# Attention, sample attention, merge and output norm in one block, with SBUF places set by hand

## What is computed

```python
h = layer_norm(x)                                   # T = 2048 + 32 rows of 1024
x_a, B, C, z_a, q, k, v, f, z_b, merge = split(h @ w_in)
y_a = B * causal_depthwise_conv3(C * x_a) * silu(z_a)
logits[t, s] = q_t . k_s / 8 + sum of log f over s < j <= t, for s <= t   # 8 heads of 64
y_b = (softmax(logits) @ v) * silu(z_b)
mixed = sigmoid(merge_A) * (y_a @ w_proj_a) + sigmoid(merge_B) * (y_b @ w_proj_b)
y = layer_norm(2 ** 0.25 * h + mixed @ w_out)
```

## Time and profile before

| | us |
|---|---|
| median of 3 runs (lowest, highest) | 2121.68 (2120.96, 2125.2) |
| own time of the profiled execution | 2120.03 |
| its span, first to last instruction | 2117.9 |
| TensorE busy in it | 1912.2 (90%) |
| VectorE, ScalarE, GpSimd busy | 1267.0, 870.7, 402.9 |
| mean granted TensorE clock | 0.957 of full |

### The profile page before, as it was taken

How to read it: one execution, slowest core, us unless ns; L and a number is a source line. 1 busy time by engine, 2 the same in 40 slices (tenths; PEclk the granted TensorE clock), 3 DMA queues, 4 the chain that set the end, 5 groups by cost and what they waited for, 6 DMA issues and landing times. The chain is left out here.

```text
span 2117.9 us, 29147 instructions
## 1 busy us (share of the span) xinstructions
PE 1912.2 (90%) x10726; PEld 1750.7 (83%) x10726; DVE 1267.0 (60%) x2002; ACT 870.7 (41%) x1546; POOL 402.9 (19%) x301
## 2 busy tenths in 40 slices
PE   2999999999999999999976999999993869997997
PEld 2999999999999999999974777777772659996886
DVE  7688887944646555445436888888874322225544
ACT  4454545633434344233321766676672510003221
POOL 4000110000101000000000245444453322421222
PEclk9999999999999999999985999999996779998999
DMA  4588888969789878788857155555424379436441
GB/s 176 180 307 306 291 302 280 315 227 312 254 279 327 272 242 274 243 300 277 266 193 155 36 121 118 114 121 107 100 51 103 115 282 328 153 121 216 156 149 67
DMA packets 272981, 435.99 MB, mean 206 GB/s; under 512 B 63228, under 2 KB 139404, under 8 KB 268708
## 3 DMA queue, kind: packets, MB, share of 16 engines
q1 hardware_dynamic: 272852, 434.29, 64.5%
HBM read 285.31 MB, written 148.78 MB: 205 GB/s over the span
## 5 line engine op out<-in xcount | busy, mean ns | idle before, releaser
L621 ACT ACTIVATE fr_wq<-fr_raw 128x512 fp32r<-128x512 f32 x288 | 177.9, 625 | 198.1 <-PE fr_d L518 130.7
L1482 DVE TENSOR_TENSOR at_p_lo<-at_p,at_p_hi 128x512 fp32r<-128x512 f32 (+2 forms) x240 | 195.0, 819 | 55.3 <-ACT at_p_hi L1436 54.7
L1435 ACT ACTIVATE at_p<-at_s 128x512 f32<-128x512 f32 (+1 forms) x320 | 170.5, 533 | 108.6 <-PE at_s L1359 62.9
L516 PE MATMUL fr_a<-fr_xh,fr_wq 128*128 128x348 f32 x576 | 187.7, 326 | 18.9 <-ACT fr_p L717 17.1
L516 PE MATMUL fr_b<-fr_xh,fr_wq 128*128 128x348 f32 x576 | 188.8, 328 | 17.0 <-DVE fr_u L1007 14.6
L866 DVE TENSOR_TENSOR fr_wq<-fr_raw,fr_wq 128x512 fp32r<-128x512 f32 x288 | 192.7, 683 | 10.5 <-ACT fr_wq L621 6.7
L1489 DVE TENSOR_REDUCE at_piece_max<-at_m 128x1 f32<-128x512 f32 (+2 forms) x294 | 171.1, 603 | 37.1 <-PE at_m L1391 17.0
L516 PE MATMUL fr_c<-fr_xh,fr_wq 128*128 128x348 f32 x576 | 186.3, 323 | 1.4 <-DMA fr_wq<-w_mixed 1.4
L517 PE MATMUL fr_b<-fr_xl,fr_wq 128*128 128x348 f32 x576 | 186.7, 324 | 0.0
L517 PE MATMUL fr_a<-fr_xl,fr_wq 128*128 128x348 f32 x576 | 186.7, 324 | 0.0
L518 PE MATMUL fr_a<-fr_xh,fr_wq 128*128 128x348 f32 x576 | 186.7, 324 | 0.0
(11 more groups left out here) (303 smaller groups left out, 4821.4 us busy)
## 6 DMA issues: line engine op xcount, KB each, us to landing
fr_wq<-w_mixed SPq DMA_DIRECT2D x192, 512.0 KB, 5.5
fr_raw<-w_tiles SPq DMA_DIRECT2D x96, 512.0 KB, 5.4
w_mixed<-fr_wq SPq DMA_DIRECT2D x96, 512.0 KB, 4.3
mg_gates<-merge_gates SPq DMA_DIRECT2D x40, 416.0 KB, 4.1
fr_raw<-w_tiles SPq DMA_DIRECT2D x48, 256.0 KB, 5.5
merge_gates<-fr_res SPq DMA_DIRECT2D x32, 348.0 KB, 6.7
mixed<-mg_mixed SPq DMA_DIRECT2D x40, 208.0 KB, 2.8
ln_m<-mixed SPq DMA_DIRECT2D x16, 512.0 KB, 4.0
```

What stands on the lines that cost most here:

```text
L516: pe.matmul(to, wh[:, idx, k, :], xh[:, idx, k, :], start=first, stop=False, skip_group_check=skip)
L621: act.activation(wh[:, idx], operand(i, idx), ACT.Copy).then_inc(w_hi[idx], 1)
L1435: act.activation(p[:, r, cols], s_bank[r][:, cols], ACT.Exp, scale=SCALE)
L1482: dve.tensor_tensor(p_lo[:, r, cols], p[:, r, cols], p_hi[:, r, cols].bitcast(F32), ALU.subtract)\
```

## The change

The four stages become objects whose engine programs are called one after the other inside one block (`rest`), so no engine waits for all others between them; each wait is on the semaphore of what it needs. `Place` puts each buffer at an offset in SBUF, counted in float32 words, so that a stage's buffers lie where those of the one before are free: `k_rows` over attention's `main` of the even heads, `v_rows` over `k_rows`, and so on. PSUM banks are shared in the same way.

- Attention: GpSimd's part of `low` goes to VectorE, so GpSimd only finishes heads, without the waits for p_hi between. The last head's `scale`, `gate` and `lower` go from VectorE to GpSimd.
- SP loads the sample's small inputs in head 1 (`early_loads`) and the four pieces of K, all of them resident, in head 7 (`key_loads`). VectorE makes the sample's masks before head 1, GpSimd clears its queries at the start.
- `tail_loads` is SP's order from there on. V pieces are loaded when the K piece in their place is turned.
- The kT parts take two slots instead of whole buffers. Merge's item (0, 0, 0) is issued on TensorE before the sample's last transposes; merge's first weight splits stand inside the sample part.
- w_out is loaded and split during merge's second group, in two raw buffers; output uses four pairs of banks, four slots of m and no special first tiles. Loops are written out.

```diff
-    prompt_attention(nc, held, s, ident, causal)
-    sample_attention(nc, held, s, cache_k, cache_v, ident, causal, blocks)
-    merge(nc, held, s, wpa_tiles, wpb_tiles)
-    output_norm(nc, held, s, w_out, ln_out, y_prompt, y_sample)
+    rest(nc, held, s, cache_k, cache_v, ident, causal, blocks, wpa_tiles, wpb_tiles, w_out, ln_out, y_prompt, y_sample)
...
+class Place:
+    BASE = 16512
+    def __init__(self, nc, tag):
+        self.nc, self.tag = nc, tag
+    def __call__(self, name, shape, at, dt=F32):
+        return self.nc.alloc_sbuf_tensor_at(f"{self.tag}_{name}", list(shape), dt, offset=self.BASE + 4 * at)
+def rest(nc, held, s, cache_k, cache_v, ident, causal, blocks, wpa_tiles, wpb_tiles, w_out, ln_out, y_prompt, y_sample):
+    with ExitStack() as ctx:
+        att = prompt_attention(nc, held, s, ident, causal)
+        sam = sample_attention(nc, held, s, att, cache_k, cache_v, blocks)
+        mrg = merge(nc, held, s, att, sam, wpa_tiles, wpb_tiles)
+        out = output_norm(nc, held, s, mrg, w_out, ln_out, y_prompt, y_sample)
+        block = ctx.enter_context(nc.Block())
+        @block.sync
+        def _(sp):
+            att.sync(sp, sam)
+            tail_loads(sp, s, att, sam, mrg, out)
+        @block.tensor
+        def _(pe):
+            att.tensor(pe)
+            sam.tensor(pe, mrg)
+            mrg.tensor(pe)
+            out.tensor(pe)
+        @block.scalar
+        def _(act):
+            att.scalar(act)
+            sam.scalar(act, mrg)
+            mrg.scalar(act, out)
+            out.scalar(act)
+        @block.vector
+        def _(dve):
+            att.vector(dve, sam)
+            sam.vector(dve)
+            mrg.vector(dve, out)
+            out.vector(dve)
+        @block.gpsimd
+        def _(pool):
+            att.gpsimd(pool, sam)
+            sam.gpsimd(pool, mrg)
+            mrg.gpsimd(pool)
+            out.gpsimd(pool)
...
+        main = sb("main", [P, 2, 4, SEQ], 0, F32R)
+        km = sb("km", [HR, 3, SEQ], 16384, F32R)
+        qm = sb("qm", [HR, 3, SEQ], 22528, F32R)
...
-                pe.wait_ge(*low_value(h, st))
+                pe.wait_ge(lo_done, NS * h + st + 1)
...
+            for h in range(1, H):
                 for st in range(NS):
-                    if st % POOLS == POOLS - 1:
-                        low(h, st)
-                    if before and st in FINISH_LOW:
-                        lower(h - 1, 1 - b, FINISH_LOW[st])
-                    if before and st in FINISH and FINISH[st][1] < 2:
-                        (scale, gate)[FINISH[st][1]](h - 1, 1 - b, FINISH[st][0])
-            for h in range(H):
-                head(h, h % 2)
-def sample_attention(nc, held, s, cache_k, cache_v, ident, causal, blocks):
+                    if st in FINISH_LOW:
+                        lower(pool, h - 1, 1 - h % 2, FINISH_LOW[st])
+                    if st in FINISH and FINISH[st][1] < 2:
+                        (scale, gate)[FINISH[st][1]](pool, h - 1, 1 - h % 2, FINISH[st][0])
...
+        def key_loads(sp):
+            sp.wait_ge(*att.head6_done)
+            for c in range(NP):
+                sp.dma_start(k_rows[:, c], cache_k[c * PIECE:(c + 1) * PIECE, :].rearrange("(b p) c -> p b c", p=P))\
+                  .then_inc(k_in[c], 16)
+            for i in range(2):
+                sp.dma_start(ck[i * H:(i + 1) * H, :].bitcast(F32), s["ck"][i, :, SEQ:SEQ + PAST]).then_inc(past_in, 16)
+            sp.dma_start(pick32[:, :], blocks).then_inc(pick_in, 16)
+        def load_v(sp, c):
+            sp.wait_ge(turned, 4 * c + 4)
+            for d in (2 * c, 2 * c + 1):
+                sp.dma_start(v_rows[:, d], cache_v[d * 2 * P:(d + 1) * 2 * P, :].rearrange("(b p) c -> p b c", p=P))\
+                  .then_inc(v_in[d], 16)
...
+            h, b = H - 1, (H - 1) % 2
+            low_v(0)
+            low_v(1)
+            for q in range(NQ):
+                att.scale(pool, h, b, q)
+            for q in range(NQ):
+                att.gate(pool, h, b, q)
+            pool.wait_ge(*att.gated)
+            low_v(2)
+            low_v(3)
+            for q in range(NQ):
+                att.lower(pool, h, b, q)
+            pool.wait_ge(*att.lows)
+            for d in range(4, ND):
+                low_v(d)
+                if d == 5:
+                    mrg.low_w(pool, 0, 0)
+            mrg.low_w(pool, 0, 1)
...
+                    high_v(2 * c - 2)
                     copy_scores(c - 1)
+                    high_v(2 * c - 1)
             copy_scores(NP - 1)
+            high_v(2 * NP - 2)
             copy_scores(NP)
+            high_v(2 * NP - 1)
+            for q in range(NQ):
+                att.upper(act, H - 1, (H - 1) % 2, q)
...
+                if c in (0, 1):
+                    mrg.high_w(act, 0, c)
...
+                if c == 0:
+                    att.invert(dve, H - 1)
...
+            mrg.item(pe, 0, 0, 0)
...
+        def high_w(act, t, b):
+            n = 4 * t + b
+            act.wait_ge(w_in[b % 2], 32 * (n // 2) + 32)
+            if n in (2, 3):
+                act.wait_ge(*sam.all_values)
+            if n == 3:
+                act.wait_ge(sam.scored, 2 * sam.NP + 2)
+            if t:
+                act.wait_ge(proj_done, IT * t - 3 + b)
...
+                    if t == NT - 1 and (n, b) in out.LOW_AT:
+                        out.low_w(dve, out.LOW_AT.index((n, b)))
...
+        def tensor(pe):
+            pe.wait_ge(w_lo_done, KT)
+            for t in range(N):
+                rows, slot = rows_of(t), t % 4
+                if t < 4:
...
+def tail_loads(sp, s, att, sam, mrg, out):
+    h = H - 1
+    att.sum_store(sp, h, 3)
+    sam.load_v(sp, 0)
+    att.sums_load(sp, h)
+    sam.load_v(sp, 1)
+    att.rcp_store(sp, h)
+    sam.load_v(sp, 2)
+    att.rcp_load(sp, h)
+    sam.load_v(sp, 3)
+    sp.wait_ge(sam.scored, 6)
+    mrg.load_gates(sp, 0, 0, 0)
+    mrg.load_gates(sp, 0, 0, 1)
+    mrg.load_y(sp, 0, "yah")
+    sam.load_new_v(sp)
+    sp.wait_ge(sam.scored, 8)
+    mrg.load_w(sp, 0, 0)
+    mrg.load_w(sp, 0, 1)
+    for q in range(NQ):
+        att.y_store(sp, h, q)
+    for q in att.y_out:
+        sp.wait_ge(*q)
+    mrg.load_y(sp, 0, "yal", "ybh", "ybl")
+    sp.wait_ge(sam.v_lo_done, sam.ND)
+    mrg.load_y(sp, 1, *mrg.names)
+    sp.wait_ge(*sam.all_values)
+    mrg.load_gates(sp, 0, 0, 2)
+    mrg.load_w(sp, 0, 2)
+    sam.store_y(sp)
+    mrg.load_gates(sp, 0, 0, 3)
+    mrg.load_w(sp, 0, 3)
+    mrg.load_y(sp, 2, *mrg.names)
+    mrg.load_y(sp, 3, *mrg.names)
+    sp.wait_ge(sam.out, 32)
+    for n, b in mrg.items:
+        mrg.step(sp, 0, n, b)
+        if (n, b) == (0, 3):
+            mrg.load_y(sp, 4, *mrg.names)
+        if n == 1 and b < 2 or n == NCH - 1 and b >= 2:
+            mrg.load_w(sp, 1, b)
+    for n, b in mrg.items:
+        mrg.step(sp, 1, n, b)
+        if (n, b) == (0, 1):
+            out.load_w(sp, 0)
+            out.load_w(sp, 1)
+        if (n, b) == (1, 0):
+            out.load_consts(sp)
+            out.load_h(sp, 0)
+        if (n, b) in out.LOW_AT and out.LOW_AT.index((n, b)) + 2 < KT:
+            out.load_w(sp, out.LOW_AT.index((n, b)) + 2)
+        if n == 4 and b < 2:
+            out.load_m(sp, b)
+    out.load_m(sp, 2)
+    out.load_m(sp, 3)
+    out.load_h(sp, 1)
+    out.sync(sp)
```

More of the change, by code:

```diff
@@ L2163, in _ @@
[L2163 to L2180 removed]
+            for t in range(4):
+                high(t)
```

989 lines of the change are left out of this document (469 added, 520 removed).

## The result

The changed kernel takes **2044.5 us** (median of 4 runs, 2039.3 to 2046.8) against 2122.3 us (2121.0 to 2125.2, 4 runs) for the kernel before in the same session: ratio 0.9629, 95% interval 0.9617 to 0.9642. That is 78 us, or 3.7%, less. The forecast was 2052, 7.5 us too slow; its range held the time. The profiled execution took 2046.76 us with a span of 2045.0, 3.2 us under the forecast span of 2048.2. The other 4.3 us are the step from the span to the median: the forecast added 3.75 us, but this profiled execution was the slowest of its four, so that the median lies 0.5 us under its span.

The account below looks back on a forecast made before the run. Beside TensorE's own work, its waits for two first loads and w_out's split, 64.7 us, bound the kernel. 1605 + 4 + 55 + 2.6 + 183 + 2.6 + 185 + 11 = 2048.2 us of span, 2052 as median; range 2038 to 2072.

Parts of the forecast that it names:

- the three waits of 32.6, 17.4 and 14.7 us: TensorE's waits between stages for a first load, the first y load and w_out's split, 64.7 us in all.
- Attention: Subtractions moved to VectorE cost 0.7 us per head in heads 1 to 6, +4 us; bounds -8 and +26.
- lower bound of -8: Attention at best: half of the 16.4 us of row-max waits goes, since GpSimd has less in the way.
- the third rival: Attention, steps 20 to 37: GpSimd holds VectorE's subtractions, up to 28 us per head; slower than before 0.03, 2074 us 0.05.
- The sample part: From attention's end to the end of the sample's values: 55 us, bounds 50 and 65.
- GpSimd's chain: Sample part: first scale at 19 us, then finishing operations and splits to 51, last values 2 us later.
- The 26 us for four pieces of K: Sample part: four K pieces at the 6.5 us that transposes and scores took at full clock.
- Merge: 40 items at full clock, 183 us, with 2 us of stall (0 to 8) at item 2 and 0.6 for transposes.
- Output: Same 816 matmuls, bound by TensorE: 187 us at 0.99 of the clock, so 185.
- The first: Rival: low clock in the sample part, four K pieces at about 10 us instead of 6.5, +14, 2066 us; chance 0.10.
- The second: Rival: loads take the waits' place, rcp_all later +6, y0 later +10, both +16, 2058 to 2068 us; chance 0.09.
- The fourth: Rival: attention gains 8 us and the sample part ends at 50, 2039 us; chance 0.04.

Follow-up runs that it names:

- experiment 1: The kernel before with all 40 subtractions of a head on VectorE, GpSimd only finishing heads: 2113.6 us, ratio 0.9955.
- experiment 4: The changed kernel with GpSimd's scale and gate of heads 0 to 6 on 8 of each 512 columns: 2022.7 us in one run.
- Experiments 7 and 8: The changed kernel with merge weight loads (0, 2), (0, 3) ahead of y1's: 2039.2 us; then also (1, 2), (1, 3) an item earlier: 2032.8 us.
- Experiment 9: The changed kernel with four merge weight loads issued earlier and output's first m_lo split made at merge's last item but one: 2029.9 us.
- experiment 3: The changed kernel with GpSimd's finishing operations spaced by waits for every fourth step's exponential, without subtractions: 2048.8 us, ratio 0.9653.
- experiment 5: The changed kernel with K's pieces, forget rows and picks loaded after attention's last sum_store instead of in head 7: 2067.3 us, ratio 0.9726.
- experiment 10: The 2029.9 us version with the reciprocal at step 5 instead of 9 and finishing operations from step 14 instead of 20: 2033.4 us.

## Why the prediction was right, and where it was wrong

That the total came within 7.5 us of 2044.5 is in part luck. The idle stretches between the stages went as forecast and for the reason given; but attention's -13.7 us and merge's +9.8 us against the forecast cancel for the most part, and neither size was foreseen.

**What bounded the kernel.** Right: the three waits of 32.6, 17.4 and 14.7 us are gone but for 2.4. K's and w_out's early loads are worth 20.6 and 26.7 us in the changed kernel, measured by taking each back, K's together with the small loads behind it and w_out's with an output that waits for all its slices.

**Attention.** This term was wrong in sign: +4 us forecast, -9.7 measured (its end at 1595.3 instead of 1605.0), beyond its own lower bound of -8. The count of the cost was near: VectorE has 51.6 us of work in head 2 instead of 49.5, and in steps 16 to 31 25.6 of 25.7 us, where 26.4 of 26.5 was forecast; the 0.08 us by which its operations overlap is in the trace of the kernel before, where a reduction from 1290.89 to 1291.58 is followed by a subtraction at 1291.49. What failed is the step that gave nothing back for the subtractions which leave GpSimd, beyond "the other 12 are no longer spaced and come in threes". The table shows TensorE's time in attention (idle is the length less the busy time of the windows):

| kernel | length | busy | idle |
|---|---|---|---|
| before | 450.4 | 426.5 | 23.9 |
| before, subtractions moved | 441.0 | 426.7 | 14.3 |
| changed | 440.1 | 425.5 | 14.6 |
| changed, every fourth moved back | 450.7 | 426.6 | 24.1 |
| changed, finishing spaced | 446.7 | 431.7 | 15.0 |
| changed, scale and gate narrow | 414.4 | 414.4 | 0.0 |

Moving the subtractions alone gives the gain and moving them back alone undoes it. Busy time hides one thing: the kernel before has four stretches of 3.4 us at half clock in attention (from 1257.3, 1373.4, 1547.5 and 1588.4), the changed kernel none. The clock isn't the main part, though: heads 2, 4 and 5, at full clock in both, fell from 57.9 each to 56.9, 56.4 and 57.2, while heads 1, 3 and 6 with such a stretch had taken only 0.6, 0.4 and 0.2 us more than 57.9. With the 1.7 us of head 7 that makes the clock's part some 3 of the 10 us, an estimate that no run separates. In head 2, the 22 subtractions were held 22 x (895 - 682) = 4.7 us by 18 GpSimd operations on 512 columns, 0.26 us for each; 28 are held 28 x (806 - 682) = 3.5 us by 12, 0.29 each. So six operations fewer give VectorE back 1.2 us there, and the two small operations of the turn end 1.0 us sooner (0.99 + 0.17 us instead of 0.92 + 1.18), which TensorE waits for directly. Its wait at the turn of head 2 fell by 2.0 us (2.2 to 0.2), of which the head kept 1.0, since waits for single row-max pieces grew from 1.0 to 1.5 us and busy time by 0.6. The forecast counted half of the turn's wait as the most that could return; 11.8 of 16.4 us did.

Head 0, which was to stay, fell by 1.1 us (55.5 to 54.4), with its ten GpSimd subtractions gone too. Head 7 was forecast to stay and fell by 1.8 us, 46.27 to 44.43, in the changed kernel and in experiment 1; with the subtractions back it took 46.5. The kernel before and the one with subtractions back each show a stretch of 3.4 us at half clock in that head, at a wait of 1.5 us for p_lo; the two others don't. That fits the size (1.7), and wasn't tried by itself.

That GpSimd's work holds VectorE's subtraction is in the traces: at 512 columns it took 895 ns in the mean in head 2 beside 18 GpSimd operations of 512 columns, 806 beside 12, and 690 in experiment 4, where GpSimd was busy for only 7.3 us of the head. The longest, 3005 ns, ran in the kernel before from 1585.51 to 1588.51, while three GpSimd operations followed each other without a gap from 1585.00 to 1589.64. But the mean cost to the subtraction was 0.26 to 0.29 us per GpSimd operation, in all 3.5 to 4.7 us per head, where the third rival, built on this single longest case, put 28. The prediction named two SBUF inputs as what makes the difference; the last section shows an operation with one that was held as well, 0.92 us instead of 0.17.

**The sample part.** Right: 53.7 us against 55, and GpSimd's chain as worked out (19.6 us to the first scale against 19). The 26 us for four pieces of K took a full clock for granted that the kernel before did not show there: it was at 0.50 from 1608.9, within the idle stretch, to 1656.7, and the 6.5 us for one piece are from a row at 0.88. The changed kernel has 1.00 until 1622.6, with 26.1 us of TensorE's work for the pieces and the new keys, where 27.3 and 4 of waits were forecast. One detail was not foreseen: ScalarE's four upper operations of the last head (2.27 us) stand between the shift and the first exponential, TensorE waits 4.6 us there, where the kernel before waited 2.3, and a stretch of 10.2 us at half clock begins within the wait, worth 3.0. The shift, ready at 28.3 instead of 32, paid for it. The prediction named a longest wait for rcp_all's chain as a sign of being wrong. It was close to that: the last `upper` starts at 1624.87, just when GpSimd's last `gate` ends (1624.84), so a later chain would have held the exponentials as well.

**Merge.** The term that was sized wrong. The mechanism was forecast: (0, 2) lies behind y1's loads and its splits are late. It took 5.7 us, not 2. Counted from attention's end, the load was forecast to land at 63 and item 2 to be wanted at 64.8; it landed at 65.7 (the split on ScalarE starts at 1661.03) and the item was wanted at 63.6. So it came 2.7 later for a reader 1.2 earlier. The loads of y1 were issued at 51.1 to 52.8, as forecast (51.5); what was sized too small is the weight's own way behind them, 11.1 us from its issue at 54.6. To that come a second wait at item 23, 2.7 us where the kernel before had 1.4, and the half-clock stretches behind both, 2.9 and 1.7. In all 3.7 + 1.3 + 2.9 + 1.7 = 9.6 of the 9.8 us. Experiments 7 and 8 took all of it back: merge at 183.2.

**Output.** 187.1 instead of 185: the stretch at half clock behind the m_lo wait, 1.7 us. The kernel before has one at the same place (0.50 from 1909.3 to 1922.9), and the forecast had scaled its 187 to full clock though a wait ahead of output stays. Experiment 9 shows 185.4 at 1.00 without the wait.

**The rivals.** The first, low clock in the sample part, came about in one stretch (0.91 instead of 0.76), but cost 3 us, not 14. The second, loads that take the waits' place, is what happened at item 2, with 3.7 us more instead of 6 to 16, and in merge, not in the sample part. The fourth had the right sign for attention and came nearest of the rivals: 2039, since it had only one of the two misses. Nothing ended on the side of slower. Of the signs by which the prediction was to be known, sa_t's start (0.1 us after the last at_o), the first merge matmul (53.7) and the wait for m_lo (2.4) came; a head of 58 to 59.5 us with VectorE over 52 busy and a turn's wait over 2.2 did not (57.0, 51.6 and 0.2), nor did a wait of 1 to 4 us at item 2 (5.7).

## What to carry to other kernels

When operations with two SBUF inputs leave GpSimd for VectorE, count what GpSimd's absence gives back, not only what VectorE takes on: here ten more subtractions a head, six of them of 0.68 us or more, on a VectorE that had little room made heads 1 to 6 0.7 to 1.5 us shorter, since TensorE waited for the small operations behind them. Where a low-clock stretch stands behind a short wait of TensorE, price the wait at itself plus half of the busy time of that stretch, an estimate from matmuls that came every 0.43 us in it instead of 0.23: waits of 2.4 and 5.7 us cost 4.1 and 8.6 so. Look in the trace whether there is one: a stretch at 0.50 stood behind all six turn waits of 1.2 us in experiment 3, but behind only three of the six of 2.2 us in the kernel before, and behind none of the waits of 1.7 and 1.9 us at merge's item 8. When loads are moved, count the small ones behind the large: picks of 16 KB held the sample part for 8.7 us in experiment 5. And when first loads are moved ahead of a stage, look at which one is wanted second and third: the order within the queue (a weight of 512 KB behind 3.3 MB of y) was worth 6 us of merge's length.

## What the runs showed of the hardware

Three instructions on 16 columns, on which TensorE's turn waits, in the kernel before, and GpSimd beside them:

```profile
1313.47 0.22 DVE L1496 TENSOR_REDUCE at_row_max<-at_piece_max 128x16 f32<-128x64 f32 x1
1313.72 0.92 DVE L1498 TENSOR_SCALAR at_neg_max<-at_row_max 128x16 fp32r<-128x16 f32 x1
1314.68 1.18 DVE L1500 SCALAR_TENSOR_TENSOR at_neg_max<-at_row_max,at_neg_max 128x16 fp32r<-128x16 f32 x1
```
```profile
1313.35 1.26 POOL L1257 TENSOR_TENSOR at_y_lo<-at_y,at_y_hi 64x512 fp32r<-64x512 f32 x1
1314.58 1.25 POOL L1253 TENSOR_TENSOR at_y<-at_y,at_zb 64x512 f32<-64x512 f32 x1
```

and the same two of VectorE in experiment 10, where GpSimd has no work at that time:

```profile
1312.33 0.17 DVE L1512 TENSOR_SCALAR at_neg_max<-at_row_max 128x16 fp32r<-128x16 f32 x1
1312.54 0.18 DVE L1514 SCALAR_TENSOR_TENSOR at_neg_max<-at_row_max,at_neg_max 128x16 fp32r<-128x16 f32 x1
```

An operation of 0.17 or 0.18 us took 0.92 or 1.18 us here when a GpSimd operation had begun just before it: it ended where that one ended (1314.64 and 1314.61; 1315.86 and 1315.83). The one with a single SBUF input was held as well (0.92), while the reduction with one was not (0.22, beside GpSimd's operation from 1313.35 to 1314.61). So these small operations weren't spared for their size: what they paid was the rest of GpSimd's operation. Head 2 of the changed kernel shows it once more: the first of the two takes 0.99 us and ends at 1313.15, GpSimd's at 1313.12, and the second, behind it, takes 0.17.

Short transfers issued behind large ones in SyncE's queue landed late. In experiment 5 the sums' 8 KB landed in 1.7 us as a median and in 8.4 when issued behind K's 4 MB and 1 MB of V, and the picks' 16 KB landed 11.3 us after their issue behind K (11.0 in the changed kernel, which issues them behind K too, but at 1570.3, so that VectorE's conversion of them at 1596.2 had no wait for them).
